# Three pieces of dense work moved ahead across two stage seams, and the hand-written order of a recurrence shifted by one part

## What is computed

```python
h = jnp.concatenate([meta, x], axis=1)                    # 16 + 1024 rows
u = rmsnorm(h, mix_norm_pre[l])
proj = u @ w_in[l]
q, f_logit, i_in, g_out, v_pool, gate_a, gate_b = jnp.split(proj, cuts, axis=-1)
a = hgrn2(q, f_logit, i_in, g_out, lbs[l], hgrn_out_norm[l])   # chunked recurrence
p = multiscale_pool(v_pool, pool_proj[l], pool_scale[l])
z = (jax.nn.sigmoid(gate_a) * (a @ w_branch_hgrn[l])
     + jax.nn.sigmoid(gate_b) * (p @ w_branch_pool[l]))
```

## Time and profile before

| | us |
|---|---|
| median of 3 runs | 2998.55 |
| lowest and highest | 2994.99, 3000.08 |
| the profiled execution, its own time | 3001.69 |
| its span in the profile | 3000.0 |
| PE busy | 2771.5 (92%) |
| DVE, ACT, POOL busy | 1679.4, 1185.1, 512.6 |

### The profile page before, as it was taken

How to read it: one execution, slowest core, us unless ns; L and a number is a source line. 1 busy time by engine, 2 the same in 40 slices (tenths; PEclk the granted TensorE clock), 3 DMA queues, 4 the chain that set the end, 5 groups by cost and what they waited for, 6 DMA issues and landing times. The chain is left out here.

```text
span 3000.0 us, 38389 instructions
## 1 busy us (share of the span) xinstructions
PE 2771.5 (92%) x14590; PEld 2417.3 (81%) x14590; DVE 1679.4 (56%) x2114; ACT 1185.1 (40%) x1714; POOL 512.6 (17%) x298
## 2 busy tenths in 40 slices
PE   9989999898899999989998999898999499999993
PEld 7989999798788998978776889666776388888883
DVE  5357654361444344333434732665533699999996
ACT  4343333321311111112334212554432377777774
POOL 3000000003121221200100000002610134444441
PEclk9999999999999999999998999999999699999997
DMA  5342332343111111113423121112302399999996
GB/s 193 101 128 92 106 95 72 120 124 126 70 43 49 49 42 49 49 49 98 142 76 106 43 57 64 36 50 85 112 25 106 140 398 419 416 412 416 416 415 241
DMA packets 244298, 436.92 MB, mean 146 GB/s; under 512 B 21698, under 2 KB 180690, under 8 KB 218594
## 3 DMA queue, kind: packets, MB, share of 16 engines
q1 hardware_dynamic: 234690, 400.88, 37.2%
q0 software_dynamic: 9504, 34.61, 2.9%
HBM read 375.54 MB, written 59.90 MB: 145 GB/s over the span
## 5 line engine op out<-in xcount | busy, mean ns | idle before, releaser
L3451 DVE TENSOR_TENSOR k_w_lo<-k_raw,k_w_hi 128x2048 fp32r<-128x2048 f32 x192 | 433.4, 2289 | 41.0 <-ACT k_w_hi L3387 37.4
L3387 ACT CAST k_w_hi<-k_raw 128x2048 fp32r<-128x2048 f32 x192 | 362.9, 1910 | 67.1 <-PE bank L3307 41.3
L120 PE MATMUL bank<-u_ffn_hi,f_w_hi 128*128 128x342 f32 (+1 forms) x840 | 294.1, 350 | 5.7 <-POOL f_w_lo L1331 5.7
L122 PE MATMUL bank<-u_ffn_hi,f_w_lo 128*128 128x342 f32 (+1 forms) x840 | 294.5, 351 | 0.0
L121 PE MATMUL bank<-u_ffn_lo,f_w_hi 128*128 128x342 f32 (+1 forms) x840 | 294.1, 350 | 0.0
L120 PE MATMUL bank<-u_hi,p_w_hi 128*128 128x342 f32 (+2 forms) x720 | 236.7, 329 | 8.9 <-DVEq L880 6.0
L121 PE MATMUL bank<-u_lo,p_w_hi 128*128 128x342 f32 (+2 forms) x720 | 231.1, 321 | 0.0
L122 PE MATMUL bank<-u_hi,p_w_lo 128*128 128x342 f32 (+2 forms) x720 | 230.8, 321 | 0.0
L3305 PE MATMUL bank<-k_w_hi,k_x_hi 128*128 128x512 f32 x512 | 203.8, 398 | 5.4 <-DVE k_x_lo L3457 5.1
L3307 PE MATMUL bank<-k_w_hi,k_x_lo 128*128 128x512 f32 x512 | 200.6, 392 | 0.0
L3306 PE MATMUL bank<-k_w_lo,k_x_hi 128*128 128x512 f32 x512 | 200.3, 391 | 0.0
(11 more groups left out here) (564 smaller groups left out, 6752.7 us busy)
## 6 DMA issues: line engine op xcount, KB each, us to landing
k_raw<-in_w_e_gate_dram SPq DMA_DIRECT2D x64, 1024.0 KB, 7.0
k_raw<-in_w_e_up_dram SPq DMA_DIRECT2D x64, 1024.0 KB, 7.6
k_raw<-in_w_e_down_dram SPq DMA_DIRECT2D x64, 1024.0 KB, 8.1
d_raw<-in_ffn_w_down_dram SPq DMA_DIRECT2D x44, 512.0 KB, 3.3
p_w<-in_w_in_dram SPq DMA_DIRECT2D x34, 512.0 KB, 4.3
f_raw<-in_ffn_w_gate_dram SPq DMA_DIRECT2D x22, 512.0 KB, 3.7
f_raw<-in_ffn_w_up_dram SPq DMA_DIRECT2D x22, 512.0 KB, 3.7
gate_scratch<-g_out SPq DMA_DIRECT2D x20, 513.0 KB, 6.2
```

Source lines behind the costliest of these rows:

```text
L120: pe.matmul(out, wh[:, t, :], xh[t][:, c:c + n], start=t == 0, stop=False)
L122: m = pe.matmul(out, wl[:, t, :], xh[t][:, c:c + n], start=False, stop=t == tiles - 1)
L3387: act.copy(wh[:, q, :], raw[:, r, :]).then_inc(hi_made, 1)
L3451: dve.tensor_tensor(wl[:, q, :], raw[:, r, :], wh[:, q, :], ALU.subtract).then_inc(lo_made, 1)
```

## The change

The first input tile (n = 0, an f tile) is computed at the end of PE's list in `stage_load`. The first two gate parts are computed at the end of PE's list in `stage_hgrn_in`. In `stage_recur` four parts instead of three come before the first scores, two of them done already, and the lists of PE, ACT, DVE (`low_at`) and SP (`weights`) follow by one slot. SP's `store` line stays as it was. So slot i does part i + 4, and `weights(m + 4)` now stands at i = 3m, ahead of `store(m - 1)` in the same slot. `keep(2)` with `high(2)` behind it comes before the exponentials of chunk 0.

```diff
@@ stage_load
+def input_tile(pe, bank, n, w, u):
+
+    for j, (c, size) in enumerate(REAL):
+        m = product(pe, bank[3 * (n % 2) + j][:, 0:size], (w[0][:, n % 2], w[1][:, n % 2]), [tiles_of(b) for b in u], c, size)
+    return m
...
             values(BLOCKS - 1)
+            pe.wait_ge(first_lo, 1)
+            pe.wait_ge(vec_kept, 1)
+            pe.wait_ge(high_kept, BLOCKS)
+            input_tile(pe, bank, 0, early, u)
...
-                        dve.tensor_tensor(early[1][:, n], raw[:, n, :, :], early[0][:, n], ALU.subtract)
+                        dve.tensor_tensor(early[1][:, n], raw[:, n, :, :], early[0][:, n], ALU.subtract).then_inc(first_lo, 1)
...
-            dve.tensor_copy(vec[:, :], bank[0][:, 0:2 * P])
+            dve.tensor_copy(vec[:, :], bank[0][:, 0:2 * P]).then_inc(vec_kept, 1)
@@ stage_hgrn_in
-            for n in range(TILES):
-                high, low = early if n < 2 else (wh, wl)
+            pe.sem_inc(mm, 1)
+            for n in range(1, TILES):
                 if n >= 2:
                     pe.wait_ge(lo_made, n - 1)
                     pe.wait_ge(taken, n - 1)
-                for j, (c, size) in enumerate(REAL):
-                    m = product(pe, bank[3 * (n % 2) + j][:, 0:size], (high[:, n % 2], low[:, n % 2]), u, c, size)
-                m.then_inc(mm, 1)
+                input_tile(pe, bank, n, early if n < 2 else (wh, wl), u).then_inc(mm, 1)
+            pe.wait_ge(lo_made, TILES - 1)
+            for e in range(FIRST_DONE):
+                gate_part(pe, bank, e, (wh, wl), u)
@@ stage_recur
-FIRST_PARTS = 3
+FIRST_PARTS = 4
+FIRST_DONE = 2
...
+def gate_part(pe, bank, e, w, u):
+
+    n, to, c, size = part(e)
+    return product(pe, bank[6 + e % 2][:, 0:size], (w[0][:, n % 2], w[1][:, n % 2]), [tiles_of(b) for b in u], c, size)
...
-                if (i + 11) % 3 == 0 and (i + 11) // 3 < GATE_TILES:
-                    weights((i + 11) // 3)
+                if (i + 12) % 3 == 0 and (i + 12) // 3 < GATE_TILES:
+                    weights((i + 12) // 3)
...
-                n, to, c, size = part(e)
                 if e % 3 == 0:
-                    pe.wait_ge(lo_made, n + 1)
-                if e >= 2:
-                    pe.wait_ge(kept, e - 1)
-                product(pe, DENSE[e % 2][:, 0:size], (wh[:, n % 2], wl[:, n % 2]), u, c, size).then_inc(dmm, 1)
+                    pe.wait_ge(lo_made, e // 3 + 1)
+                pe.wait_ge(kept, e - 1)
+                gate_part(pe, bank, e, (wh, wl), u).then_inc(dmm, 1)
...
-            for e in range(FIRST_PARTS):
+            pe.sem_inc(dmm, FIRST_DONE)
+            for e in range(FIRST_DONE, FIRST_PARTS):
                 dense(e)
...
-                if (i + 5) % 3 == 0 and 2 <= (i + 5) // 3 < GATE_TILES:
-                    low((i + 5) // 3)
+                if (i + 6) % 3 == 0 and 2 <= (i + 6) // 3 < GATE_TILES:
+                    low((i + 6) // 3)
```

More of the change, by code:

```diff
@@ L189, in first_column @@
     return HALF + t if kind == "f" else t
+def input_tile(pe, bank, n, w, u):
+    for j, (c, size) in enumerate(REAL):
+        m = product(pe, bank[3 * (n % 2) + j][:, 0:size], (w[0][:, n % 2], w[1][:, n % 2]), [tiles_of(b) for b in u], c, size)
+    return m
 def stage_load(nc, ctx, A, K, bank, h0, u, h0_dram, v_d, raw, w_in, early):
     (meta_in, gain_in, rows_in, rows_zero, ident_zero, ident_made, eps_made, made, turned, squared, rstd_made, scaled, x_turned, xn_turned, low_kept,
-     high_kept, u_hi, u_lo, stored, first_hi, wv_hi, wv_lo, vmm, v_kept, v_out0, v_out1, zeros_made, zeros_out) = sems(
+     high_kept, u_hi, u_lo, stored, first_hi, first_lo, vec_kept, wv_hi, wv_lo, vmm, v_kept, v_out0, v_out1, zeros_made, zeros_out) = sems(
         ctx, nc, "l", "meta_in gain_in rows_in rows_zero ident_zero ident_made eps_made made turned squared rstd_made scaled x_turned xn_turned low_kept "
-        "high_kept u_hi u_lo stored first_hi wv_hi wv_lo vmm v_kept v_out0 v_out1 zeros_made zeros_out")
+        "high_kept u_hi u_lo stored first_hi first_lo vec_kept wv_hi wv_lo vmm v_kept v_out0 v_out1 zeros_made zeros_out")
     wv_in = sems(ctx, nc, "l", " ".join(f"wv_in{g}" for g in range(HALF)))
@@ L635, in gate_column, with is_pool, part @@
     return 5 * HALF + n - 2 * HALF
+def is_pool(n):
+    return n < 2 * HALF and n % 2 == 0
+def part(e):
+    n, j = e // 3, e % 3
+    c, size = REAL[j] if is_pool(n) else LIVES[j]
+    return n, c, (c if is_pool(n) else SKIP + c), size
+def gate_part(pe, bank, e, w, u):
+    n, to, c, size = part(e)
+    return product(pe, bank[6 + e % 2][:, 0:size], (w[0][:, n % 2], w[1][:, n % 2]), [tiles_of(b) for b in u], c, size)
 def stage_recur(nc, ctx, A, K, bank, u, q_d, k_d, lf_d, v_d, o, sig_d, pool_d, raw, wh, wl):
@@ L676, in halves @@
             return v[:, :, 0, :], v[:, :, 1, :]
[L678 to L685, removed]
         def head(h):
@@ L3551, in program @@
                         stage_load(nc, ctx, A, K, bank, h0, u_pair, h0_d, v_d, raw, w_in, early)
-                    u_pair = [tiles_of(b) for b in u_pair]
                     wh, wl = (buffer(weights, nc, n, [P, 2, KD, P], F32R, side="right") for n in ("p_w_hi", "p_w_lo"))
```

## The result

The changed kernel took 3034.95 us (median of 4 runs, 3032.08 to 3037.72), the kernel before 2999.32 (median of 4, 2994.99 to 3003.55) on the same occasions: a ratio of 1.0126, 95% interval 1.0108 to 1.0144, 35.6 us slower. 29 were forecast, 3027.6. The time lies in the wide range of 3012 to 3037, but outside the 3022 to 3032 that the forecast gave itself; the mechanism is the one forecast, and the sum was 7 us too small. The profiled execution took 3033.56, its span is 3031.8.

What follows compares the result with a forecast made beforehand. PE's work plus its holes was taken to set the time; -2.1 + 2.0 + 2.1 + 2 x (8.4 + 3.7 + 3.2) - 3.8 = +28.8, say +29, gave 3027.6 us against the median 2998.55, range 3022 to 3032, wide range 3012 to 3037.

Steps and rivals of the forecast that it cites:

- The stores: Recurrence: SP's stores, now behind the weights, land late and stall PE six times, 2 x (8.4 + 3.7 + 3.2) us.
- first seam: End of the load stage: matmuls fill PE's hole, so tile 1 starts at 89.75 instead of 94.10, -4.35 us.
- both seams and the start, to slot 4: Up to slot 4: recurrence starts 2.1 us earlier, but late weight tile 2 and what follows cost +2.0.
- slot 4's part 8 behind `pool(0)`: Slot 4: part 8 needs `keep(6)`, which needs `pool(0)`, now standing behind `low(3)`: +2.1 us.
- slots 31 and 55: Stall counted from slots 24 and 48: store of tile 9 kept at 45.6, part 35 due at 42.4, +3.2 us each.
- the pairs: Counted from slots 11 and 35: parts 17 and 18 late by 0.7 and 3.0 us, +3.7 each pair.
- the long stalls: Counted from slots 24 and 48: late store makes part 29 stall 6.9 us, plus 1.5 for the clock, +8.4 each.
- The others (...) come out within 0.2 of due: 0: Stores at slots 18, 27, 42, 51, and 9, 33, 57: within 0.2 us of due, no cost.
- more falls of the clock: Rival, 15 in 100: stalls of 3.0 and 3.2 us also drop PE's clock, four more at 1.5, +35, 3033.6.
- The row against the rule: ACT's table loads: 1.28 us without the skill's 1.38 drain; rival with the drain, 1 in 100, +40, 3039.
- The faster rival: Rival, 4 in 100: weight tile 2 and stores land before they are asked for, leaving -5.9 us, 2992.7.
- The forecast's own line: PE's clock: low after 3.35 us idle, not after 2.92; the stalls of 3.0 and 3.2 lie in between.

Runs made afterwards that it cites:

- e1: The changed kernel with SP's store moved one slot like the other lists, again ahead of the weights: 2996.24 us, ratio 0.9992 to the kernel before.
- e3: The kernel before with only the store moved one slot later, behind the weights, no seam touched: 3033.14 us, ratio 1.0119.
- e2: The changed kernel with the store at slot 3m but as first entry of that slot in SP's list: 2994.9 us, ratio 0.9983.
- e4: The changed kernel with three parts instead of four ahead of the first scores and the recurrence's lists as before: 2993.2 us, ratio 0.9977.
- e7: e1 with the rounding of weight tile 2 moved behind the exponentials of chunk 0: 2990.55 us, ratio 0.9967 to the kernel before.
- e6: The kernel before with only the first seam's edit, the f tile at the end of the load stage: 2995.17 us, ratio 0.9982.
- e5: The changed kernel with the weights last in each slot of SP's list, the store behind the chunk loads: 3004.03 us, ratio 1.0016.

## Where the prediction failed: 7 us short in "The stores", with the mechanism right

By its own steps, at the end of the recurrence, where it had +28.8 and the trace shows +35.8 (the first row is contained in the second):

| step | predicted | trace |
|---|---|---|
| first seam | -4.35 | -4.59 (tile 1 at 89.51) |
| both seams and the start, to slot 4 | -0.1 | -0.72 |
| slot 4's part 8 behind `pool(0)` | +2.1 | +2.0 |
| slots 25 and 49 | +8.4 each | +9.1, +8.45 |
| slots 13 and 14, 37 and 38 | +3.7 each | +5.6, +5.7 |
| slots 31 and 55 | +3.2 each | +3.2, +2.4 |
| all other slots | 0 | +3.6 |
| slot 68 | -3.8 | -3.8 |

- **The mechanism was right**: which line was left behind, which slots stall most, in what order the waits follow each other. The exponentials were to begin 13.55 into the stage and began at 13.2; the store of slot 24 was to land at 11.9, and ACT went on at 11.6. e1 and e3 show that the line is the cause.
- **The step that failed is "The stores", in two of its terms.** First, the pairs, +3.7 each, measured 5.6 and 5.7. Their second hole (slots 14 and 38) is 2.64 where 3.0 was expected, but PE came back from it at the low clock, and the slot lost 4.3; slot 31, which came back at the high clock from a hole of 2.92, lost 3.2, or 0.3 more than its hole. So the low clock took some 1.4 of the 4.3, and the sum had priced the clock for the long stalls only. The first stall of each pair (slots 13 and 37) cost 1.4 where 0.7 was expected.
- Second, **"The others (...) come out within 0.2 of due: 0"**. They cost 3.6: slots 46 and 58 1.5 each, slot 52 0.5. Slots 52 and 58 hang on the stores of slots 51 and 57, which it names. Slot 46 hangs on the store of slot 45, which its list leaves out, as it does 15, 21 and 39; those three cost nothing. Slot 46's part needs `keep(48)`, which follows the exponentials, and the table load of this `keep` stood behind the wait for the store, so 1.28 came on top. ACT's timeline there:

```profile
446.38 2.86 ACT L936 ACTIVATE scaled_chunk<-scaled_chunk 128x1536 f32<-128x1536 f32 x2
...
453.34 1.28 ACT L964 ACT_TABLE_LOAD   x1 [2.53 <-DMA gate_scratch<-g_out]
```

- In slot 58 PE waited for the store of tile 18. It went out at 520.65, 2.0 into slot 56, and ACT had it 9.2 later, not 6.3; PE idled 1.25 there (530.33), so by an estimate from these numbers it would have been in time with 6.3:

```profile
529.82 0.80 ACT L964 ACTIVATE g_out<-bank 128x342 f32<-128x342 f32 x2 [10.37 <-DMA gate_scratch<-g_out]
```

- Why this landing was slower stays open.
- The +8.4 of the long stalls was near for a reason that it did not have. Counted in the same way (hole and 0.3, the rest for the clock), the stalls themselves are some 6.6 and 6.5, not 6.9, and the clock took 2.5 and 1.9, not 1.5. Two misses of opposite sign met there.
- The rival "more falls of the clock" had the right kind, and its 3033.6 lies near the measured time by luck: two of its four falls came, and other slots made up the rest. It drew its line through idle times, and the shorter hole fell while the longer one in slot 31 did not.
- **The table load.** The row against the rule held: in the changed kernel the load at 189.45 takes 1.28 and the exponentials begin at 190.74, 0.01 later. The Trainium skill's drain of about 1.38 us behind each load (ScalarE: Activation LUTs, What ACT_TABLE_LOAD costs) does not appear in this trace.
- **The faster rival** needed the stores and weight tile 2 in time. It did not happen, but e2, e4 and e7 show what it was worth: with the stores in time the same seams give 4 to 10 us.
- No run shows a cost of either seam's edit. Most of the gain is the first seam's: slot 0 begins 3.8 earlier with it alone (e6), 4.5 with both (e4).

## What to carry to other kernels

A schedule written by hand in four lists is one schedule. Whoever moves three of them by a step has moved the fourth by a step the other way, and a transfer that hid behind an idle engine may come out on the bound one. Before a shift, look for the longest harmless wait (here ACT's 7.08 us for a store), and count how many steps lie between it and the engine that sets the time. In an in-order queue that issues transfers, put those whose work is long done ahead of those that still wait for work, and keep a load that isn't needed yet from standing in front of the first step of a chain.

## What the hardware showed that was not expected

**The clock after holes of about 3 us is not decided by the length of the hole.** In the changed kernel PE idled 2.64 in front of slot 14's part, 2.92 in front of slot 31's. The stretches behind the first hole and behind the second (columns: PE, PEld, DVE, ACT, POOL, then PE's granted clock):

```profile
272.00:274.00 2.00, 1.96 (x7) 1.99 (x8) 0.79 (x1) 1.17 (x2) 0.00 (x0) 0.50 0.00 0
...
371.90:374.00 2.10, 2.06 (x13) 2.06 (x14) 2.10 (x8) 0.82 (x2) 0.00 (x0) 1.00 0.00 0
```

The shorter hole was followed by the low level (0.50, 1.2 GHz), the longer one by the high (1.00, 2.4 GHz). In slot 3, the same code left the same hole in the kernel before, in e3 and in e6. Before, the clock stayed high. The lines of e3 and of e6:

```profile
212.01 0.63 PE L120 MATMUL bank<-u_hi,p_w_hi 128*128 128x352 f32 x1 [2.90 <-ACT g_out L944]
```

```profile
208.00 0.63 PE L120 MATMUL bank<-u_hi,p_w_hi 128*128 128x352 f32 x1 [2.92 <-ACT g_out L961]
```

Both lost 2.7 to 2.8 there against before. e6 ran at the low level for some 6 us, busy all the while, and e3 did the same:

```profile
208.00:210.00 2.00, 2.00 (x7) 2.00 (x8) 1.02 (x2) 1.14 (x2) 0.00 (x0) 0.50 0.43 172
210.00:212.00 2.00, 2.00 (x9) 2.00 (x8) 0.39 (x1) 0.00 (x0) 0.00 (x0) 0.50 0.11 24
212.00:214.00 2.00, 2.00 (x8) 2.00 (x7) 0.00 (x0) 0.00 (x0) 0.00 (x0) 0.50 0.80 186
```

In e5, after 2.89 of idle time, PE came back at the high clock, and the clock fell only while it was busy again (0.93, then 0.50):

```profile
328.30:330.00 1.70, 1.66 (x10) 1.66 (x11) 0.00 (x0) 0.83 (x2) 0.00 (x0) 0.93 0.65 261
330.00:332.00 2.00, 2.00 (x9) 2.00 (x9) 0.00 (x0) 0.00 (x0) 0.00 (x0) 0.50 0.00 0
```

The forecast's own line, low after 3.35 us in front of tile 0, was one execution too. In e3 the same hole came back at the high clock, and the fall (0.50 from 83 to 85 us) came behind it:

```profile
80.99 0.40 PE L120 MATMUL bank<-u_hi,p_first_hi 128*128 128x352 f32 x1 [3.35 <-PEq L206]
```

So a hole near 3 us cost either little more than itself or, in these traces, 1.6 to 2.8 us more, and one profiled execution does not tell which for the next. The Trainium skill (TensorE: Matmul & The Clock Gate, Part 1) says that the number of matmuls at the low clock differs from run to run of the same kernel, and these rows agree.

**A table load can stand on either side of a wait.** Before the exponentials ACT loads its table and then waits (178.70 and 186.77 in e4). Before `keep(48)` in the changed kernel it waited for the store and then loaded (453.34). Where the wait is long, the first hides the 1.28 us and the second adds them.
